# Roots chunk by chunk, half the tokens through the norms first, and a recurrent mixer in two halves of heads

## The reference, cut to what matters

```python
def mixer_rglru(h, w_in, conv_w, conv_b, w_a, b_a, w_x, b_x, lam, w_out):
    gate, xr = jnp.split(h @ w_in, [D_RNN], axis=-1)
    gate = jax.nn.gelu(gate)
    xr = causal_conv(xr, conv_w) + conv_b
    xh = xr.reshape(bsz, t_len, LRU_HEADS, LRU_HEAD_DIM)          # 8 heads of 128
    r = jax.nn.sigmoid(einsum('bthi,hij->bthj', xh, w_a) + b_a)
    i = jax.nn.sigmoid(einsum('bthi,hij->bthj', xh, w_x) + b_x)
    log_a = (LRU_C * r) * jax.nn.log_sigmoid(lam)
    a = jnp.exp(log_a)
    b = jnp.sqrt(-jnp.expm1(2.0 * log_a)) * (i * xr)
    hseq = scan of h[t] = a[t] * h[t-1] + b[t]
    return (gate * hseq) @ w_out

def rms_norm(x, g):
    return x * lax.rsqrt(jnp.mean(jnp.square(x), axis=-1, keepdims=True) + EPS) * g
```

## Time and profile before

| | us |
|---|---|
| median of three runs | 2706.59 (2702.04 to 2707.36) |
| the profiled execution: its time | 2703.67 |
| its span, first to last instruction | 2702.3 |
| TensorE busy | 2592.2 (96%) |
| VectorE busy | 1148.7 (43%) |
| ScalarE busy | 899.4 (33%) |
| GpSimd busy | 360.3 (13%) |

### The profile page before, as it was taken

The page is one execution under the profiler, slowest core; times in us unless marked ns, Lnnn a source line. Parts: engine busy times, 40 slices in busy tenths (PEclk is TensorE's granted clock), DMA queues, the critical chain, the costliest instruction groups (busy, mean ns, idle before and its releaser), DMA issues.

```text
span 2702.3 us, 33251 instructions
## 1 busy us (share of the span) xinstructions
PE 2592.2 (96%) x13432; PEld 1818.3 (67%) x13432; DVE 1148.7 (43%) x2169; ACT 899.4 (33%) x1740; POOL 360.3 (13%) x165
## 2 busy tenths in 40 slices
PE   7998999999998899999979999999999999999999
PEld 6875444444766444444467778888888777888887
DVE  2543323332646332232256343562554534365254
ACT  3431111111464111111154554442345445443233
POOL 3200000000331000000021011222222001122222
PEclk9999999999898999999989999999999999999999
DMA  5229999999311999999932011223231201223212
GB/s 198 79 81 418 419 422 421 421 421 418 118 62 57 419 419 421 421 421 420 421 122 79 32 63 48 94 94 110 68 113 59 79 33 62 79 94 109 78 63 86
DMA packets 139003, 543.28 MB, mean 201 GB/s; under 512 B 18784, under 2 KB 30304, under 8 KB 89696
## 3 DMA queue, kind: packets, MB, share of 16 engines
q1 hardware_dynamic: 129232, 536.94, 50.8%
q10 hardware_dynamic: 9616, 4.18, 0.6%
HBM read 538.99 MB, written 2.10 MB: 200 GB/s over the span
## 4 chain that ended last, share of the span: by engine, by line
PE 90%; DVE 5%; ACT 2%; issue 2%; DMA 0%; POOL 0%; SPq 0%; DVEq 0%; ACTq 0%
PE ps L603 23%; PE ps L1363 16%; PE ps L605 14%; PE ps L1385 8%; PE ps L1338 5%; PE ps L625 4%; PE ps L537 4%; PE ps L1398 3%; PE ps L1939 2%; PE ps L1399 2%; PE ps L1912 2%; PE ps L1931 1%; PE ps L538 1%; PE ps L455 1%; DVE w L278 1%
## 5 line engine op out<-in xcount | busy, mean ns | idle before, releaser
L603 PE MATMUL ps<-w,w 128*128 128x512 f32 x2976 | 679.9, 390 | 2.6 <-POOL w L278 2.6
L603 PEld LDWEIGHTS ps<-w,w 128*128 128x128 f32 x2976 | 559.0, 188 | 119.7 <-POOL w L278 3.4
L278 POOL TENSOR_TENSOR w<-w,w 128x1024 fp32r<-128x1024 f32 (+2 forms) x139 | 337.2, 2435 | 2182.9 <-ACT w L270 2182.9
L1363 PE MATMUL ps<-w,w 128*64 128x512 f32 x2048 | 451.6, 594 | 1.8 <-issue 1.8
L605 PE MATMUL ps<-w,w 128*128 128x512 f32 (+1 forms) x1872 | 410.9, 381 | 18.2 <-issue 15.2
L270 ACT ACTIVATE w<-w 128x1024 fp32r<-128x1024 f32 (+2 forms) x260 | 252.7, 1001 | 436.2 <-PE ps L603 196.9
L605 PEld LDWEIGHTS ps<-w,w 128*128 128x128 f32 x1872 | 339.9, 189 | 85.5 <-issue 19.7
L278 DVE TENSOR_TENSOR w<-w,w 128x1024 fp32r<-128x1024 f32 (+2 forms) x121 | 200.7, 1666 | 386.8 <-ACT w L270 384.4
L1363 PEld LDWEIGHTS ps<-w,w 128*64 128x64 f32 x2048 | 146.0, 137 | 285.6 <-issue 285.6
L1615 DVE TENSOR_TENSOR X<-ps,X 128x512 f32<-128x512 f32 x256 | 163.0, 682 | 163.0 <-PE ps L1399 161.9
L1385 PE MATMUL ps<-w,w 128*64 128x512 f32 x1024 | 226.8, 595 | 0.8 <-ACT w L1449 0.8
(11 more groups left out here) (251 smaller groups left out, 2325.3 us busy)
## 6 DMA issues: line engine op xcount, KB each, us to landing
w<-in_moe_w_gate SPq DMA_DIRECT2D x128, 1024.0 KB, 14.0
w<-in_moe_w_up SPq DMA_DIRECT2D x128, 1024.0 KB, 16.4
w<-in_moe_w_down SPq DMA_DIRECT2D x128, 1024.0 KB, 13.0
w<-in_w_up SPq DMA_DIRECT2D x40, 1024.0 KB, 5.1
w<-in_w_down SPq DMA_DIRECT2D x20, 1024.0 KB, 5.1
w<-in_w_in SPq DMA_DIRECT2D x16, 1024.0 KB, 5.1
w<-in_ab_w_in SPq DMA_DIRECT2D x10, 1024.0 KB, 5.1
w<-in_c_w_in SPq DMA_DIRECT2D x8, 1024.0 KB, 5.1
```

Of the source, the lines that this page charges most:

```text
L278: up(self.wlo[self.low[s][0]], lane.e.tensor_tensor(lo, raw, hi.bitcast(F32), ALU.subtract))
L603: ins = pe.matmul(bank[:, :], wp[:, k, P * o:P * o + P], ap(k0 + k), start=first, stop=stop)
L1363: ins = pe.matmul(bank[64 * e:64 * e + 64, :], XG[p % 3][:, 4 * u + k, 64 * e:64 * e + 64], w[e][:, k, :], start=(u == 0 and k == 0), stop ...
```

## The change

- `scalar_squares` takes one root for each chunk, and `vector_norm` one reciprocal for each chunk.
- Behind the first layer of experts only chunks 0 and 1 are squared and scaled in `moe`; chunks 2 and 3 follow in the mixer, between the two halves of the rows.
- VectorE's wait for the roots stands inside the overflow loop.
- `middle_norm` takes chunks 0 and 1 through both norms, then 2 and 3 through the first; their second norm follows behind the first half of the rows. `turn` sets which root VectorE waits for.
- The mixer runs by halves of four heads: gate matrices of heads 0 to 3, first half of the gate, gate matrices of heads 4 to 7, second half of the gate. The gate matrices become two units. For heads 0 to 3 the square goes to the gate's tile (`GT[0]`), which is filled later. The last two conversions of the x branch stand behind the first four decays.

```diff
     def scalar_squares(ready, chunks=range(NT)):
         for c in chunks:
             ready(c)
             square(X[:, c, :], D, SM[:, c:c + 1])
-            if c == 1:
-                scalar_roots(0, 2, D)
-            if c > 1:
-                scalar_roots(c, 1, D)
+            scalar_roots(c, 1, D)
...
     def plan_lru():
         w = A["c_w_in"][0]
-        for key, c0 in ((("xr", 0), 1024), (("xr", 1), 1536), (("gt", 0), 0)):
-            plan_cols(key, w, c0, 512)
-        W.add("gates", [(8, 128, A["c_w_a"][0].rearrange("h i j -> i h j")),
-                        (8, 128, A["c_w_x"][0].rearrange("h i j -> i h j"))], split=False)
-        plan_cols(("gt", 1), w, 512, 512)
+        for s in range(2):
+            plan_cols(("xr", s), w, 1024 + 512 * s, 512)
+        for s in range(2):
+            W.add("gates", [(4, 128, A[name][0][4 * s:4 * s + 4].rearrange("h i j -> i h j")) for name in ("c_w_a", "c_w_x")],
+                  split=False)
+            plan_cols(("gt", s), w, 512 * s, 512)
...
         def scalar():
-            scalar_rows(rows, None, late, False)
+            scalar_rows(rows, last_square, late, False)
...
+                scalar_product(("xr", s), taps_in, tail=2 * s)
+
+            def decays(hs):
+                for h in hs:
+                    for dst, bias in ((RB, "c_b_a"), (IB, "c_b_x")):
+                        bank = ba.next(S)
+                        bank_to(dst[:, h, :], bank[:, :], ACT.Sigmoid, bias=col(bias, h))
+                S.wait_ge(lam_ready, 1)
+                for h in hs:
+                    S.wait_ge(i_x, h + 1)
+                    up(a_exp, act.activation(AA[:, h, :], RB[:, h, :], ACT.Exp, scale=SM[:, 32 + h:33 + h]))
+                    S.wait_ge(a_exp, h + 1)
+                    if h > 3:
+                        S.wait_ge(x_conv, h + 1)
+                    up(ss, act.activation(squared(h), AA[:, h, :], ACT.Square))
+                    up(a_sq, act.activation(RB[:, h, :], RB[:, h, :], ACT.Tanh, scale=SM[:, 80 + h:81 + h]))
+
+            def roots(hs):
+                for h in hs:
+                    S.wait_ge(q_done, h + 1)
+                    up(b_root, act.activation(RB[:, h, :], RB[:, h, :], ACT.Sqrt))
...
+            decays(HEADS[0])
+            for h in behind_gates:
+                W.hi(h)
+            scalar_product(("gt", 0), gelu_0, second=lambda: roots(HEADS[0]))
+            decays(HEADS[1])
+            roots(HEADS[1])
             for m in range(4):
                 S.wait_ge(y_mult, m + 1)
...
         def vector():
+            factors(HEADS[0])
+            for h in behind_gates:
+                W.lo(h, V)
+            vector_product(("gt", 0), second=lambda: scans(HEADS[0]))
+            factors(HEADS[1])
+            scans(HEADS[1])
+            for m in range(4):
+                low(m)
             vector_product(("gt", 1))
...
         def gpsimd():
+            inputs(HEADS[0])
+            for h in behind_gates:
+                W.lo(h, G)
+            gpsimd_product(("gt", 0))
+            inputs(HEADS[1])
             for m in range(4):
-                G.wait_ge(ba.free, 8 + m + 1)
+                G.wait_ge(ba.free, 8 + 8 + m + 1)
...
     def moe(layer, last_square, last_norm, next_half, next_norm):
-            scalar_squares(lambda c: S.wait_ge(bx.free, 8 * (PAIRS - 1) + 2 * c + 2))
+            scalar_squares(whole, range(ahead))
...
             if next_norm:
-                vector_norm(next_norm, ((0, 2),))
+                vector_norm(next_norm, ((0, 1), (1, 1)))
             vector_combine(3)
-            if next_norm:
-                vector_norm(next_norm, ((2, 1), (3, 1)))
...
-        V.wait_total(rt, rt.n)
         nblocks = nc.values_load(NI[0:1, 0:1], min_val=0, max_val=2 * T // CAP)
...
+                dve.wait_ge(rt.h, rt.n)
                 vs_(dve.tensor_scalar(OH, OS, BC, None, ALU.is_le))
...
-        return late
+        if not next_norm:
+            return late
+        return late, lambda: scalar_squares(whole, (2, 3)), lambda: vector_norm(next_norm, ((2, 1), (3, 1)))
...
     def middle_norm(rows):
         def vector():
             V.wait_dma(W.s_raw[unit.slot], unit.arrived)
-            groups = ((0, 2), (2, 1), (3, 1))
-            vector_norm(apply, groups)
+            vector_norm(apply, ((0, 1), (1, 1)), first)
+            vector_norm(norm_of_rows(rows), ((0, 1), (1, 1)), second)
+            vector_norm(apply, ((2, 1), (3, 1)), first)
             W.raw_consumed_at[unit.n] = (xw, xw.n)
-            vector_norm(norm_of_rows(rows), groups[:1])
-            return lambda: vector_norm(norm_of_rows(rows), groups[1:])
+            return lambda: vector_norm(norm_of_rows(rows), ((2, 1), (3, 1)), second)
         last_norm = vector()
-        scalar()
-        return None, last_norm
+        squares((0, 1))
+        return lambda: squares((2, 3)), last_norm
```

More of the change, by code:

```diff
@@ L917, in vector @@
             apply = norm_of_rows(rows)
-            vector_norm(apply, ((0, 2),))
+            vector_norm(apply, ((0, 1), (1, 1)))
             vector_half(rows, 0)
@@ L1012, in mixer_rglru, with squared @@
         YL = at(20480, 8, 512, dt=F32R)
-        gates = W.of["gates"][0]
         H = rows.H
+        HEADS = (range(0, 4), range(4, 8))
+        behind_gates = late_halves(("xr", 1), 2)
+        def squared(h):
+            return GT[0][:, h, :] if h < 4 else XT[:, h - 4, :]
         def tensor():
             tensor_first_product(rows, ("xr", 0), 4, 512, ba, True)
[L1018 to L1028, removed]
+            tensor_product(("xr", 1), ALL4, 512, H, ba, feature=True)
+            for s in range(2):
+                gates = W.of["gates"][s]
+                wg = W.need_raw(gates, PE)[:, 0:1024].rearrange("p (g h j) -> p g h j", g=2, h=4)
+                for h in HEADS[s]:
+                    PE.wait_ge(x_conv, h + 1)
+                    for g in range(2):
+                        bank = banks.take(ba)
+                        n = up(ba.full, pe.matmul(bank[:, :], wg[:, g, h % 4, :], XC[:, h, :], start=True, stop=True))
+                W.raw_consumed_at[gates.n] = (ba.full, n)
+                tensor_product(("gt", s), ALL4, 512, H, ba, feature=True)
             tensor_out("lruo", (lambda k: YH[:, k, :], lambda k: YL[:, k, :]), lambda k: PE.wait_ge(ylo, k),
@@ L1041, in taps_in @@
                         bank_to(XT[:, o, :], bank[:, :])
[L1042 to L1045, removed]
-                    bank = ba.next(S)
[L1047 to L1058, removed]
@@ new lines, in roots, with gelu_0 @@
+            def roots(hs):
+                for h in hs:
+                    S.wait_ge(q_done, h + 1)
+                    up(b_root, act.activation(RB[:, h, :], RB[:, h, :], ACT.Sqrt))
+            def gelu_0():
+                for o in range(4):
+                    bank = ba.next(S)
+                    S.wait_ge(q_done, 1 + o)
+                    bank_to(GT[0][:, o, :], bank[:, :], ACT.Gelu_apprx_tanh)
+            decays(HEADS[0])
+            for h in behind_gates:
+                W.hi(h)
@@ L1082, in vector @@
         def vector():
-            vector_rows(rows, None, late, False)
+            vector_rows(rows, last_norm, late, False)
             log_sigmoid_in(cols("c_lambda", 0, 8), SM[:, 40:48])
@@ L1101, in taps, with factors, scans @@
                         up(x_conv, ins)
[L1102 to L1106, removed]
+                vector_product(("xr", s), taps, tail=2 * s)
+            def factors(hs):
+                for h in hs:
+                    V.wait_ge(a_sq, h + 1)
+                    up(q_done, dve.scalar_tensor_tensor(RB[:, h, :], squared(h), 1.0, RB[:, h, :], ALU.add, ALU.mult))
+            def scans(hs):
+                for h in hs:
+                    V.wait_ge(b_root, h + 1)
+                    V.wait_ge(i_x, h + 1)
+                    vstep(dve.tensor_tensor(IB[:, h, :], IB[:, h, :], RB[:, h, :], ALU.mult))
+                    up(scanned, dve.tensor_tensor_scan(RB[:, h, :], AA[:, h, :], IB[:, h, :], 0.0, ALU.mult, ALU.add))
             def low(m):
@@ L1129, in gpsimd, with inputs @@
             gpsimd_late(late)
[L1130 to L1134, removed]
+            for s in range(2):
+                gpsimd_product(("xr", s), tail=2 * s)
+            def inputs(hs):
+                for h in hs:
+                    G.wait_ge(ba.free, 8 + 4 * (h // 4) + 2 * h + 2)
+                    up(i_x, pool.tensor_tensor(IB[:, h, :], IB[:, h, :], XC[:, h, :], ALU.mult))
+            inputs(HEADS[0])
[3 more added lines that the diff above has]
+            inputs(HEADS[1])
             for m in range(4):
-                G.wait_ge(ba.free, 8 + m + 1)
+                G.wait_ge(ba.free, 8 + 8 + m + 1)
                 G.wait_ge(scanned, m + 1)
@@ L1449, in bank_to_free, with whole @@
             up(ch.free, act.activation(dst, bank, ACT.Copy))
+        added = bx.free.base
+        def whole(c):
+            S.wait_total(bx.free, added + 8 * (PAIRS - 1) + 2 * c + 2)
```

(5 more changed lines are left out.)

27 lines of the change are left out of this document (10 added, 17 removed).

## The result

The changed kernel took 2680.15 us (median of four executions, 2677.77 to 2684.47) against 2706.07 us before: ratio 0.9909, 95% interval 0.989 to 0.9927. The forecast was 2682.5, in a range of 2676 to 2693. The profiled execution took 2677.77 us (span 2676.0), 25.9 less than the one of before.

What follows compares the result with a forecast made beforehand. TensorE, busy 96% of the span, was taken as the bound. Terms 17.7 + 1.2 + 3.7 = 22.6 us gave 2681.1 from the profiled execution and 2684.0 from the median; the middle, 2682.5, was forecast, range 2676 to 2693.

Steps and rivals of the forecast that it cites:

- Mixer, 17.7: Mixer by halves of heads: pause before the output product shrinks by 14.6 us, that product by 3.1; 17.7 us.
- the walk: Instruction-by-instruction timing of engine queues; in the mixer, first `low` at 806.0 against TensorE's arrival at 805.8, leaving 0.6 us.
- Rival 1: ScalarE becomes the mixer's bound, slipping 7 us: 13.1 us gained in place of 22.6, time 2692; chance 0.17.
- First boundary, 1.2: Behind the first experts: the first product waits for the transposes alone, 698.7 against 699.89, 1.2 us; bounds -1 to 3.
- slow clock that ends sooner: Behind the first experts: part of the upper bound of 3 us, beside the whole 1.55 us wait.
- Second boundary, 3.7: Behind the second experts: earlier norms and no wait before the branch gain 3.7 us, bounds 2.4 and 4.5.
- the branch: Behind the second experts: VectorE's branch without the wait costs 0 to 1.0 us; middle taken, first reciprocal at 1373.0.
- Rival 2: Both boundaries give nothing because GpSimd's conversions delay norms 2 and 3; mixer alone, 2687.4 us; chance 0.11.
- Start, 0: First stage: the earlier norm is hidden by TensorE's 4.40 us wait for GpSimd's first weight conversion; gain 0.
- Rivals 3 and 4: Mixer: wait moves ahead of second gates or gate product, 2701 to 2705 (0.06); output weights load late, slower (0.04).
- some 110 us: Whole kernel: all that can be won, claimed to be TensorE's idle time and its slow stretches.

Runs made afterwards that it cites:

- loads_behind: The changed kernel with two more table loads on ScalarE behind the mixer's last sigmoid; 2685.01 us, ratio 0.993.
- filler: The changed kernel with transposes of the identity filling TensorE's pauses around the experts; 2672.95 us, ratio 0.9882.

## Why the prediction was right, step by step

**Mixer, 17.7: right, measured 17.8.** The changed kernel reached its first gates 4.83 us earlier than the walk had it; taken off, the walk's ends stand beside the rows so: gelu 773.1 (row: 773.03), second sigmoids 780.2 (780.01), high parts 794.7 (794.60), scans 800.5 (800.54). It held because it priced the GpSimd hold-up on the last scan at its full 2.0 us (3.31 - 1.23 = 2.08). What failed in it is a reason and not a number: that TensorE paces the second sigmoids so that loads ahead of them are free. They run back to back; the margin is about 1 us. Rival 1 was right that ScalarE has hardly any room, and wrong in its slip of 7 us. Nine table loads stand in the mixer, as forecast. That 17.7 and 17.8 lie so close is partly luck: the pause fell by 15.00 where the term has 14.6 (the walk itself left 0.2 and not 0.6), and the product by 2.83 where it has 3.10. What is left open is why a bare 12 to 16 us appear in the medians of the mixer alone, apart from the clock seen in two traces.

Two more loads made a pause of 3.19 us in `loads_behind`: a switch of tables costs what the load's row has, 1.3 us, and only where ScalarE has no room. The Trainium skill (ScalarE: Activation LUTs, section "Table sets: the hidden batching unit") has about 2.7 us for a switch, by which, as an estimate, the pause would have been 5.6; the measurement decides.

**First boundary, 1.2: right in the profiled execution, 1.3 for the stand (chain).** Transposes end at 696.16; the walk's 698.7 less 2.39, the lead at the last combine, is 696.3. The other 1.1 us came from the matmuls behind them, at the upper bound's "slow clock that ends sooner", which I had left out of the value. That the product "waits for the transposes alone" holds only where the transposes run at the lower level, as in the profiled execution. Where they run at the full clock, TensorE stands 0.67 us behind them, and the edit is worth 2.3: the forecast of 1.2 fits the lower level, and that the profiled execution had it is luck.

**Second boundary, 3.7: too small, 5.25.** The measured 5.25 lies outside the term's bounds of 2.4 to 4.5. The term that failed is the branch, taken at 0.5 us as the middle of 0 and 1.0. The row shows 0: with no wait in front, nothing of the register load and the branch stands between last add and reciprocal. Each later step of the walk came 0.5 to 1.0 earlier than forecast for it. So the walk's own 4.2 was 1.0 short, and the value stood another 0.5 below the walk, for which no row was given. Rival 2 (conversions delay the late norms) is out: no transposes of the second half wait for a norm.

**Start, 0: right**, though the first pair of traces said 2.35.

**The sum** of 22.6 became 26.3 in the trace: 17.8 + 2.4 + 5.25 from the edits, 25.5; 2.35 at the start and 0.2 between stages from the clock, less 1.7 in the second block. The clock's terms can't be forecast for one execution, so about 25 is the change. The mixer's term carries the forecast; the two boundaries were 2.8 too small together. Rivals 3 and 4: TensorE stands nowhere in the mixer but for 0.19 us, and nothing waited for the output weights: the last of them were issued at 780.3, landed within 9.6 us, and ScalarE's copies begin at 794.50. The "some 110 us" at the head of the prediction is TensorE's idle time alone (2702.3 - 2592.2); the slow stretches lie inside its busy time and come on top.

## What to carry to other kernels

A pause in front of a large product is best removed by giving its chain an earlier start on half the data; walk the one engine's queue that feeds it, instruction by instruction, with the hold-ups from other engines at full price. A wait in front of a branch that is hardly taken belongs inside it: the wait cost 2.8 us, part of it because the branch then stood behind it. And compare stage by stage, with several traces: differences of 2 to 4 us between single executions stood in stages that no edit had touched.

## What the runs showed that I had not expected

Where executions of one kernel differed and both were traced, the difference lay in TensorE's clock. One and the same kernel ran through 1570 to 1610 us at 0.96 in one execution and 0.87 in another, on another chip, and one lost 3.8 us against the other over that attention stage. After its idle times of 5.3 us in the routing (`L1355`) the clock was at the lower level in the traces of the changed kernel, 0.53 and 0.57 over the windows shown; with idle time cut to 1.3 us by transposes it stayed at 1.00. The Trainium skill (TensorE: Matmul & The Clock Gate, section "HAM oscillation — how this bites in real kernels") says that a matmul engine that waits long enough between two bursts begins the next at the low clock; these rows agree. `filler` shows that useless transposes prevent it, while the pause of 3.19 us in `loads_behind` brought no lower clock. What no run here settles is why the clock also fell in the attention, with some 3 us of idle time in the 40 us shown.
